# First block of a two-block float32 kernel: nine low weight parts a layer by accumulating transfers, a wider rotation, and the last key scalings ahead of the last rotation

## The chip, the cores and the metric

The kernel runs on one core of one Trainium2 chip. The metric is the device time of one execution in microseconds (us); the time before is the median of three runs.

The core has five engines that run their own instruction lists and wait for one another through semaphores: TensorE (PE, matrix products, with its weight loads as PEld), VectorE (DVE), ScalarE (ACT), GpSimd (POOL) and SyncE (SP, which here only issues transfers). Data comes from the chip's memory by 16 DMA engines that all issuing engines share.

## The reference

Two blocks of two layers each, on one sequence of 256 positions with 1024 features, all in float32. The change is in the first block. Its middle part, the mixer, is this (shortened):

```python
def mixer(h, w_in, ...):
    z = h @ w_in + b_in
    q, k, v, glu_in, gates = jnp.split(z, ...)        # 1536, 1536, 1536, 2048, 2048 wide
    q = apply_rope(rmsnorm(q.reshape(shp), q_norm), cos, sin)   # 24 heads of 64
    k = apply_rope(rmsnorm(k.reshape(shp), k_norm), cos, sin)
    for g, (window, dil) in enumerate(DILATION_GROUPS):
        o, l = dilated_window_attn(q[:, :, g], k[:, :, g], v[:, :, g], dil, window // (2 * dil))
    ...                                               # softmax over the three groups
    y_conv = conv_module(glu_in, conv_w, ...)         # depthwise, 31 taps a channel
    g_attn, g_conv = jnp.split(jax.nn.sigmoid(gates), 2, axis=-1)
    return (g_attn * y_attn + g_conv * y_conv) @ w_out

def first_block(x, ...):
    for l in range(DEPTH):                            # DEPTH = 2
        x = x + 0.5 * swiglu_ffn(rmsnorm(x, ffn1_norm[l]), ...)
        x = x + mixer(rmsnorm(x, mix_norm[l]), ...)
        x = x + 0.5 * swiglu_ffn(rmsnorm(x, ffn2_norm[l]), ...)
        x = rmsnorm(x, final_norm[l])
    return x
```

`apply_rope` takes the halves t1, t2 of each head to t1·cos − t2·sin and t1·sin + t2·cos.

## The kernel before

**Products.** A float32 product is made of three products of rounded parts: every weight w is split into hi (w rounded to the format fp32r) and lo = w − hi, and so is every activation. `mm3` (lines 433 to 435) adds hi·hi, hi·lo and lo·hi in PSUM.

**The weight stream.** The weights come in chunks of 128 partitions by 2048 columns (1 MB), or half of that. Chunk c lies in slot c mod 3 of three tiles: `raw` (as loaded), `hi` and `lo`. For each chunk SP issues the load (`chunk`, line 357) when the low part of chunk c − 3 is made, since that was the last reader of the slot's raw tile. ACT makes hi by a copy (`split`, line 1052) when TensorE has finished chunk c − 3. DVE makes lo by a subtraction (`split`, line 1549). TensorE waits for the count of low parts and uses the chunk. ACT and DVE split two chunks ahead of the one that TensorE is at.

**The stages of a layer's mixer**, by chunk number: 4 chunks of values (VA0), 8 of the gated unit ahead of the convolution (GLU0), 12 of queries and keys (QK0), 2 of values (V0), 8 of gates (GATE0), then projections. A chunk of queries and keys gives a pair of 128-row tiles. In QK step i:

- ACT runs `split` for chunk QK0+i+2 and then `qk_step1(i)`: when TensorE has finished chunk QK0+i it writes the pair, scaled, to `zg` (line 1157) and its squares to `zgsq` (line 1166). At i = 6 and i = 12 it also takes a square root for the norms of six pairs (line 1163).
- SP, once `zg` is there, copies it with the halves of each head exchanged to `zr` (`turn_halves`, line 367, four transfers of 64 KB).
- DVE runs `split` for chunk QK0+i+2, then `rope1(i−2)`: zg·cos (line 1708), zr·sin (line 1709) and their sum into `qk` (line 1711). It then may scale a pair by its norm (`qk_scale`, line 1719), from the norms that TensorE has spread over the partitions (lines 568 and 579). Last come six convolution taps (`some_taps`, line 1746, or 1743 for a channel tile's first tap). The 248 taps of a layer have no fixed place; they are dealt out by constants, 7 for each of six GLU steps, 6 for each QK step, 8 for each V step, 16 for each head step.

**Heads.** When six pairs are scaled, TensorE makes the first score tile (`score_pair`, line 605). Then come eight head steps t. In each TensorE runs `gates_and_values(t)`: gate chunk GATE0+t, in it the values of step t−1 (line 632), and spreads of the late six pairs' norms (`late_spread`, line 590, at k = 4 and k = 7 of the chunk's eight, by the table `late_spread_at`). Then it transposes (line 618) and makes the next scores. DVE adds the mask and takes a minimum (`scaled_min`, line 1725), splits a chunk, inverts the sums (line 1730), scales late pairs and runs taps. ACT runs the exponentials (line 1173), scales them (line 1180), splits a chunk, makes the gate (line 1266) and copies the transposed tiles (line 1185). A late spread of pair c waits until pair c−1 is scaled. At t = 6 TensorE sums the finished convolution for its norm (line 708).

GpSimd has no part in all this. The order on each engine is the order in which the code is written.

## Time and profile before

| | |
|---|---|
| time before, median of 3 runs | 2053.53 us (2047.05 to 2054.88) |
| profiled execution: its time, its span | 2046.14 us, 2044.4 us |
| granted TensorE clock over the span | 0.988 of full |
| PE busy | 1957.5 us (96%) |
| DVE busy | 1534.2 us (75%) |
| ACT busy | 1038.0 us (51%) |
| POOL busy | 0.2 us |
| chain that ended last | PE 70%, DVE 22%, ACT 5%, DMA 2% |

The busy share of PE is modelled: matmuls overlap, so a busy PE may still be short of its peak. The mixer of the first layer runs from about 205 to 520 us of the span, that of the second from about 920 to 1235 us. Both read alike, and the rows below are of the first.

### The profile page before, as it was taken

Reading aid. Unit: us, or ns where it says so; the run is one execution under the profiler, and the core shown is the slowest. Engines: PE = TensorE matmul, PEld = TensorE weight load, DVE = VectorE, ACT = ScalarE, POOL = GpSimd, SP = SyncE. Lnnn points to the kernel's source line nnn. Section 1 sums busy time; section 2 is a strip of 40 time slices with the busy share of each in tenths; the row PEclk is TensorE's granted clock in tenths of the full one; section 3 lists DMA queues with packets and bytes.
Section 4 is the critical chain, followed back from the end, with each engine's and each line's share of the span. In section 5 each row is a group of like instructions: output and inputs, shape, how many; then the busy total and the mean of one; then the engine's idle time right before and its main releaser. Section 6 shows DMA issues by size and latency. Waiting matters only on the chain.

```text
span 2044.4 us, 38994 instructions
## 1 busy us (share of the span) xinstructions
PE 1957.5 (96%) x15906; PEld 1882.4 (92%) x15906; DVE 1534.2 (75%) x2207; ACT 1038.0 (51%) x1322; POOL 0.2 (0%) x4
## 2 busy tenths in 40 slices
PE   7999999799999999999997999999999999999998
PEld 7999998688999999999987889999888999888998
DVE  6556899997765576568999977555787777878776
ACT  5444545365544454444454555444465555565554
POOL 0000000000000000000000000000000000000000
PEclk9999999899999999999998999999999999999999
DMA  6556555224555545555552236555235554334553
GB/s 246 193 185 222 190 189 188 79 76 131 207 205 185 181 142 191 194 207 200 197 181 83 73 126 231 189 185 177 94 124 175 195 185 165 135 124 165 185 185 134
DMA packets 55817, 343.38 MB, mean 168 GB/s; under 512 B 7328, under 2 KB 7584, under 8 KB 18976
## 3 DMA queue, kind: packets, MB, share of 16 engines
q1 hardware_dynamic: 54704, 339.37, 47.6%
q10 hardware_dynamic: 1008, 2.51, 0.3%
q8 instruction: 78, 1.28, 0.2%
q14 instruction: 27, 0.22, 0.0%
HBM read 334.51 MB, written 1.05 MB: 164 GB/s over the span
## 4 chain that ended last, share of the span: by engine, by line
PE 70%; DVE 22%; ACT 5%; DMA 2%; issue 1%; ACTq 0%; DVEq 0%; SPq 0%
PE bank L433 22%; PE bank L435 22%; PE bank L434 22%; DVE lo L1549 7%; DVE cv L1746 6%; ACT hi L1052 2%; DMA raw<-in_w 1%; DVE p_sb L1725 1%; DVE qk L1719 1%; DVE n_lo L1553 1%; DMA x<-in_x 1%; DVE sq L1583 0%; DVE zr L1709 0%; PE bank L821 0%; DVE zg L1708 0%
## 5 line engine op out<-in xcount | busy, mean ns | idle before, releaser
L1549 DVE TENSOR_TENSOR lo<-raw,hi 128x2048 fp32r<-128x2048 f32 (+1 forms) x336 | 715.2, 2129 | 232.8 <-ACT hi L1052 232.2
L433 PE MATMUL bank<-n_hi,hi 128*128 128x256 f32 x2256 | 637.8, 283 | 28.6 <-DVE lo L1773 12.6
L1052 ACT ACTIVATE hi<-raw 128x2048 fp32r<-128x2048 f32 (+1 forms) x336 | 597.4, 1782 | 94.8 <-PE bank L435 81.1
L434 PE MATMUL bank<-n_lo,hi 128*128 128x256 f32 x2256 | 631.7, 280 | 0.0
L435 PE MATMUL bank<-n_hi,lo 128*128 128x256 f32 x2256 | 631.5, 280 | 0.0
L433 PEld LDWEIGHTS bank<-n_hi,hi 128*128 128x128 f32 x2256 | 427.2, 189 | 34.2 <-DVE lo L1773 12.6
L434 PEld LDWEIGHTS bank<-n_lo,hi 128*128 128x128 f32 x2256 | 427.2, 189 | 1.2 <-issue 1.0
L435 PEld LDWEIGHTS bank<-n_hi,lo 128*128 128x128 f32 x2256 | 428.2, 190 | 0.0
L433 PE MATMUL bank<-h_hi,hi 128*128 128x256 f32 x1152 | 337.6, 293 | 7.3 <-DVE h_lo L1553 5.3
L434 PE MATMUL bank<-h_lo,hi 128*128 128x256 f32 x1152 | 328.6, 285 | 0.0
L435 PE MATMUL bank<-h_hi,lo 128*128 128x256 f32 x1152 | 328.3, 285 | 0.0
L433 PE MATMUL bank<-hid_hi,hi 128*128 128x256 f32 x960 | 269.1, 280 | 3.5 <-DVE lo L1549 3.5
L435 PE MATMUL bank<-hid_hi,lo 128*128 128x256 f32 x960 | 268.9, 280 | 0.0
L434 PE MATMUL bank<-hid_lo,hi 128*128 128x256 f32 x960 | 268.8, 280 | 0.0
L433 PEld LDWEIGHTS bank<-h_hi,hi 128*128 128x128 f32 x1152 | 223.4, 194 | 20.6 <-issue 14.4
L434 PEld LDWEIGHTS bank<-h_lo,hi 128*128 128x128 f32 x1152 | 223.9, 194 | 0.5
L435 PEld LDWEIGHTS bank<-h_hi,lo 128*128 128x128 f32 x1152 | 223.6, 194 | 0.0
L1746 DVE SCALAR_TENSOR_TENSOR cv<-upad,prm,cv 128x256 f32<-128x256 f32 x480 | 195.7, 476 | 0.0
L1096 ACT ACTIVATE silu_t<-up_t 128x256 f32<-128x256 f32 x88 | 36.8, 418 | 300.3 <-DVE up_t L1604 300.3
L433 PEld LDWEIGHTS bank<-hid_hi,hi 128*128 128x128 f32 x960 | 181.7, 189 | 3.9 <-DVE lo L1549 3.9
L435 PEld LDWEIGHTS bank<-hid_hi,lo 128*128 128x128 f32 x960 | 182.2, 190 | 0.0
L434 PEld LDWEIGHTS bank<-hid_lo,hi 128*128 128x128 f32 x960 | 181.6, 189 | 0.0
(242 smaller groups left out, 2225.3 us busy)
## 6 DMA issues: line engine op xcount, KB each, us to landing
raw<-in_w SPq DMA_DIRECT2D x286, 1024.0 KB, 4.8
raw<-in_w SPq DMA_DIRECT2D x53, 512.0 KB, 3.9
zr<-zg SPq DMA_DIRECT2D x96, 64.0 KB, 2.9
bv<-in_bv SPq DMA_DIRECT2D x2, 768.0 KB, 6.2
spread<-in_spread SPq DMA_DIRECT2D x2, 768.0 KB, 8.0
x<-in_x ACTq DMA_DIRECT2D x4, 256.0 KB, 10.3
out_x<-sq SPq DMA_DIRECT2D x1, 1024.0 KB, 3.9
const<-in_const ACTq DMA_DIRECT2D x1, 831.5 KB, 14.1
```

Of the source, the lines that this page charges most:

```text
L433: mm(out, w_hi, a_hi, start=start, stop=False, skip_group_check=True)
L434: mm(out, w_hi, a_lo, start=False, stop=False, skip_group_check=True)
L435: return mm(out, w_lo, a_hi, start=False, stop=True, skip_group_check=True)
L1052: fn(hi[:, s, 0:w], raw[:, s, 0:w], ACT.Copy).then_inc(sem["hi"], 1)
L1096: fn(silu_t[:, u, :], gate_of[:, u, 0, :], ACT.Silu).then_inc(sem["silu"], 1)
L1549: v.tensor_tensor(lo[:, s, 0:w], raw[:, s, 0:w], hi[:, s, 0:w].bitcast(F32), ALU.subtract)\
L1553: return v.tensor_tensor(out, full, high.bitcast(F32), ALU.subtract).then_inc(sem[name], 1)
L1719: v.tensor_tensor(t, norm_of, t, ALU.mult).then_inc(sem["qk"], 1)
L1725: v.tensor_tensor_reduce(p_sb[:, e, :], bank[3 + e][:, :], mask_f[:, u % 2, :], -(HD ** -0.5), 3e38, ALU.add, ALU.min, nmx[:, i:i + 1]).th ...
L1746: ins = v.scalar_tensor_tensor(cv[:, t, :], src, w, cv[:, t, :], ALU.mult, ALU.add)
```

## The change

**1. Nine low parts a layer are made without DVE.** For the chunks in `ADDED` (QK0+1, 3, 5, 7, 9, 11 and GATE0, GATE0+2, GATE0+4) ACT writes −hi to the slot's `lo` right after it has written hi. GpSimd then issues a transfer of the same 1 MB chunk out of memory that adds to `lo`, which gives w − hi. TensorE waits for that transfer. SP's next load into the slot waits for ACT's second copy.

**2. The rotation is one product of 1024 columns** for a pair and its turned copy, in one tile `zt` of three buffers, then the sum. The turned copy had two buffers.

**3. Order on DVE.** After a QK step whose split is gone there are 11 taps instead of 6. In the value steps pairs 4 and 5 are scaled ahead of the last rotation. The late norms' reciprocal, the third part of the values and eight taps go behind the first `scaled_min`. The late spreads are dealt out as 1, 2, 2, 1 instead of 2, 2, 1, 1, and the first waits for the values.

```diff
 def late_spread_at(t):
-    return {0: [6, 7], 1: [8, 9], 2: [10], 3: [11]}.get(t, [])
+    return {0: [6], 1: [7, 8], 2: [9, 10], 3: [11]}.get(t, [])
+ADDED = tuple(QK0 + i for i in (1, 3, 5, 7, 9, 11)) + (GATE0, GATE0 + 2, GATE0 + 4)
...
-        def chunk(c, src, half):
-            sp.wait_ge(sem["lo"], cnt.up("lo"))
+        def chunk(c, src, half, after_added=False):
+            if after_added:
+                sp.wait_ge(sem["minus"], cnt.up("minus"))
+            else:
+                sp.wait_ge(sem["lo"], cnt.up("lo"))
...
+        def take_low(c):
+            if c in ADDED:
+                take(f"added{ADDED.index(c) % 2}", 16)
+            else:
+                take("lo")
...
-                if k in (4, 7) and late:
+                if late and (k == 7 or (k == 4 and t)):
+                    if t == 0:
+                        take("v")
                     late_spread(late.pop(0))
...
-        def split(c, half=False):
+        def split(c, half=False, added=False):
...
             fn(hi[:, s, 0:w], raw[:, s, 0:w], ACT.Copy).then_inc(sem["hi"], 1)
+            if added:
+                act.wait_ge(sem["hi"], cnt.at("hi", 1))
+                fn(lo[:, s, 0:w], hi[:, s, 0:w].bitcast(F32), ACT.Copy, scale=-1.0).then_inc(sem["minus"], 1)
...
-            take(f"turn{i % 2}", 64)
-            v.tensor_tensor(zg[:, i % 3, :, :], zg[:, i % 3, :, :], cos, ALU.mult)
-            link(v.tensor_tensor(zr[:, i % 2, :, :], zr[:, i % 2, :, :], sin, ALU.mult))
+            take(f"turn{i % 3}", 64)
+            both = zt[:, i % 3, :, :, :]
+            link(v.tensor_tensor(both, both, turns, ALU.mult))
...
-            for i in range(12):
-                split(QK0 + i + 2)
-                qk_at(i)
-                some_taps(TAPS_QK)
-            for j in range(2):
-                split(V0 + j + 2)
-                qk_at(12 + j)
-                some_taps(TAPS_V)
-            for c in spread_at(13):
-                qk_scale(c)
-            add_values(2, V0 + 1)
+            for i in range(12):
+                split(QK0 + i + 2, added=QK0 + i + 2 in ADDED)
+                if i >= 2:
+                    rope1(i - 2, turns)
+                if i == QK_CHUNKS + 1:
+                    key_rstd(0)
+                for c in spread_at(i - 1):
+                    qk_scale(c)
+                some_taps(TAPS_QK + (5 if QK0 + i + 2 in ADDED else 0))
+            split(V0 + 2, added=V0 + 2 in ADDED)
+            rope1(10, turns)
+            for c in spread_at(11):
+                qk_scale(c)
+            some_taps(TAPS_V)
+            split(V0 + 3, added=V0 + 3 in ADDED)
+            for c in spread_at(12) + spread_at(13):
+                qk_scale(c)
+            rope1(11, turns)
...
             for t in range(8):
                 scaled_min(t)
+                if t == 0:
+                    key_rstd(1)
...
                 inverse_sums(t)
+                if t == 0:
+                    add_values(2, V0 + 1)
+                    some_taps(TAPS_V)
...
+    def pool_program(pool):
+            for n, c in enumerate(ADDED):
+                pool.wait_ge(sem["minus"], cnt.up("minus"))
+                pool.dma_start(lo[:, c % SLOTS, :], d["w1"][l * CHUNKS1 + c], accum_op=ALU.add)\
+                    .then_inc(sem[f"added{n % 2}"], 16)
```

**On DVE, from the second value step to the first minimum of the heads.** Here `lo<-raw,hi` is the split of chunk GATE0+1, `zg`, `zr` and `qk<-zg,zr` the rotation, `qk<-bank,qk` a pair's scaling, `cv` the taps, `rstd` the late norms' reciprocal, `v` the values. Before:

```order
L1549 TENSOR_TENSOR lo<-raw,hi 128x2048
L1708 TENSOR_TENSOR zg<-zg,const 128x512
L1709 TENSOR_TENSOR zr<-zr,const 128x512
L1711 TENSOR_TENSOR qk<-zg,zr 128x512
L1865 RECIPROCAL rstd<-std 128x256
L1719 TENSOR_TENSOR qk<-bank,qk 128x512
L1746 SCALAR_TENSOR_TENSOR cv<-upad,prm,cv 128x256 x2
L1743 TENSOR_SCALAR cv<-upad,prm 128x256 x2
L1746 SCALAR_TENSOR_TENSOR cv<-upad,prm,cv 128x256 x4
L1719 TENSOR_TENSOR qk<-bank,qk 128x512
L1760 TENSOR_TENSOR v<-bank,bv 128x512 x2
L1725 ISA p_sb,small<-bank,mask_f 128x512
```

Now:

```order
L1570 TENSOR_TENSOR lo<-raw,hi 128x2048
L1740 TENSOR_TENSOR qk<-bank,qk 128x512 x2
L1730 TENSOR_TENSOR zt<-zt,const 128x1024
L1732 TENSOR_TENSOR qk<-zt 128x512
L1746 ISA p_sb,small<-bank,mask_f 128x512
```

The reciprocal, eight taps, the values and the last rotation no longer stand ahead of the sixth pair's scaling, for which the first scores wait.

**On DVE, behind that minimum, up to the scaling of the first late pair.** Before:

```order
L1746 SCALAR_TENSOR_TENSOR cv<-upad,prm,cv 128x256 x3
L1730 RECIPROCAL small<-small 128x2
L1746 SCALAR_TENSOR_TENSOR cv<-upad,prm,cv 128x256 x3
L1719 TENSOR_TENSOR qk<-bank,qk 128x512
L1746 SCALAR_TENSOR_TENSOR cv<-upad,prm,cv 128x256 x3
```

Now:

```order
L1882 RECIPROCAL rstd<-std 128x256
L1751 RECIPROCAL small<-small 128x2
L1781 TENSOR_TENSOR v<-bank,bv 128x512 x2
L1767 SCALAR_TENSOR_TENSOR cv<-upad,prm,cv 128x256 x11
L1740 TENSOR_TENSOR qk<-bank,qk 128x512
```

What left the place above stands here, ahead of the late pairs.

**On ACT, two QK steps in a row**, `hi` being the high part and `lo<-hi` the negated copy. Before:

```order
L1052 ACTIVATE hi<-raw 128x2048
L1157 ACTIVATE zg<-bank,qk_bg,prm 128x256 x2
L1166 ACTIVATE zgsq<-bank,prm 128x256 x2
L1052 ACTIVATE hi<-raw 128x2048
L1157 ACTIVATE zg<-bank,qk_bg,prm 128x256 x2
```

Now:

```order
L1066 ACTIVATE hi<-raw 128x2048
L1069 ACTIVATE lo<-hi 128x2048
L1175 ACTIVATE zt<-bank,qk_bg,prm 128x256 x2
L1184 ACTIVATE zgsq<-bank,prm 128x256 x2
L1066 ACTIVATE hi<-raw 128x2048
L1175 ACTIVATE zt<-bank,qk_bg,prm 128x256 x2
```

Every second step has one more copy of 2048 columns, ahead of the pair that TensorE has yet to finish.

## Rows read from the trace of the kernel before

**Rows 1.** Waits of the whole kernel: total us, times, longest.

```profile
PE bank L605 <- DVE qk L1719: 20.8, 2, 10.4
```

**Rows 2.** Windows: length, busy PE, PEld, DVE, ACT, POOL, clock, DMA share, GB/s.

```profile
364.00:372.00 8.00, 3.37 (x17) 2.23 (x15) 7.96 (x15) 0.00 (x0) 0.00 (x0) 0.89 0.38 133
372.00:380.00 8.00, 2.21 (x13) 1.82 (x14) 6.93 (x13) 0.00 (x0) 0.00 (x0) 0.50 0.27 114
```

**Rows 3.** Chain that ended last, ahead of the first scores: start, duration, what.

```profile
364.61 3.17 DVE cv L1746 x8
...
377.13 0.61 DVE qk L1719
377.79 2.08 PE bank L605 x12
```

**Rows 4.** DVE in order of time, QK step 7: start, duration, instruction.

```profile
323.88 2.29 DVE L1549 TENSOR_TENSOR lo<-raw,hi 128x2048 fp32r<-128x2048 f32 x1 [1.72 <-ACT hi L1052]
326.09 0.68 DVE L1708 TENSOR_TENSOR zg<-zg,const 128x512 f32<-128x512 f32 x1
...
328.03 1.74 DVE L1865 RECIPROCAL rstd<-std 128x256 f32<-128x256 f32 x1
```

**Rows 5.** ACT in order of time: splits, and starts of a pair (TensorE just done).

```profile
268.98 1.90 ACT L1052 ACTIVATE hi<-raw 128x2048 fp32r<-128x2048 f32 x1
280.12 1.02 ACT L1157 ACTIVATE zg<-bank,qk_bg,prm 128x256 f32<-128x256 f32 x2 [2.82 <-PE bank L435]
281.75 1.93 ACT L1052 ACTIVATE hi<-raw 128x2048 fp32r<-128x2048 f32 x1
292.41 1.02 ACT L1157 ACTIVATE zg<-bank,qk_bg,prm 128x256 f32<-128x256 f32 x2 [2.98 <-PE bank L435]
294.03 1.92 ACT L1052 ACTIVATE hi<-raw 128x2048 fp32r<-128x2048 f32 x1
305.46 1.02 ACT L1157 ACTIVATE zg<-bank,qk_bg,prm 128x256 f32<-128x256 f32 x2 [2.97 <-PE bank L435]
321.93 1.92 ACT L1052 ACTIVATE hi<-raw 128x2048 fp32r<-128x2048 f32 x1
331.55 1.02 ACT L1157 ACTIVATE zg<-bank,qk_bg,prm 128x256 f32<-128x256 f32 x2 [2.98 <-PE bank L435]
```

**Rows 6.** The page's DMA issues: count, KB each, median us to landing.

```profile
raw<-in_w SPq DMA_DIRECT2D x286, 1024.0 KB, 4.8
zr<-zg SPq DMA_DIRECT2D x96, 64.0 KB, 2.9
```

**Rows 7.** Windows of 1 us behind one load's issue (columns as rows 2).

```profile
299.78:300.78 1.00, 1.00 (x11) 1.00 (x10) 1.00 (x3) 1.00 (x4) 0.00 (x0) 1.00 0.93 344
300.78:301.78 1.00, 1.00 (x10) 1.00 (x9) 1.00 (x4) 1.00 (x1) 0.00 (x0) 1.00 0.99 393
301.78:302.78 1.00, 1.00 (x11) 1.00 (x10) 0.93 (x3) 0.71 (x1) 0.00 (x0) 1.00 0.86 334
302.78:303.78 1.00, 1.00 (x11) 1.00 (x10) 1.00 (x1) 0.00 (x0) 0.00 (x0) 1.00 0.64 191
```

**Rows 8.** Chain again, in the head steps: start, duration, what.

```profile
397.97 0.61 DVE qk L1719
398.62 1.15 PE bank L590 x4
...
463.64 0.84 ACT gate L1266 x2
```

**Rows 9.** DVE in order of time behind the first scores (gap in brackets).

```profile
383.66 0.17 DVE L1730 RECIPROCAL small<-small 128x2 f32<-128x2 f32 x1 [1.15 <-ACT p_sb L1173]
...
385.63 0.69 DVE L1719 TENSOR_TENSOR qk<-bank,qk 128x512 f32<-128x512 f32 x1 [0.63 <-PE bank L590]
...
388.65 0.69 DVE L1719 TENSOR_TENSOR qk<-bank,qk 128x512 f32<-128x512 f32 x1 [1.14 <-PE bank L590]
```

**Rows 10.** A window within the head steps (columns as rows 2).

```profile
412.00:420.00 8.00, 8.00 (x75) 7.47 (x72) 8.00 (x18) 4.21 (x10) 0.00 (x0) 1.00 0.09 15
```

More of the change, by code:

```diff
@@ L402, in sp_program @@
             for c in range(VA0, FFN2_0):
-                chunk(c, d["w1"][l * CHUNKS1 + c], half_chunk_1(c))
+                chunk(c, d["w1"][l * CHUNKS1 + c], half_chunk_1(c), c - SLOTS in ADDED)
                 i = c - QK0 - 5
@@ L407, in sp_program @@
             ffn_stream(l, d["w1"], FFN2_0, CHUNKS1)
-            cnt.end(layer, dict(lo=CHUNKS1, zg=2 * QK_CHUNKS, rope=2 * QK_CHUNKS))
+            cnt.end(layer, dict(lo=CHUNKS1 - len(ADDED), minus=len(ADDED), zg=2 * QK_CHUNKS, rope=2 * QK_CHUNKS))
         for l in range(L):
@@ L445, in gates_and_values @@
             c, out = GATE0 + t, bank[GATE_BANKS[t % 2]]
-            take("lo")
+            take_low(c)
             late = late_spread_at(t)
@@ L456, in gates_and_values, with pairs @@
             last.then_inc(sem["pe"], 1)
-        def pairs(c, out, k0, nk, a_hi, a_lo, start, ready=None, stat_after=None, by_halves=False):
+        def pairs(c, out, k0, nk, a_hi, a_lo, start, ready=None, stat_after=None, by_halves=False, added=False):
             if by_halves:
                 pe.wait_ge(sem["lo0a"], 1)
+            elif added:
+                take_low(c)
             else:
@@ L681, in layer1 @@
                     pe.wait_ge(sem["u"], cnt.at("u", 6 + i))
-                pairs(c, bank[c % 3], 0, KT, h_hi, h_lo, True)
+                pairs(c, bank[c % 3], 0, KT, h_hi, h_lo, True, added=True)
                 qk_tail1(i)
@@ L691, in layer1 @@
             for t in range(8):
-                if t == 0:
-                    take("v")
                 if t >= 2:
@@ L1156, in qk_step1 @@
                     t = qk_tile(i) + j
-                    last = fn(zg[:, i % 3, j, :], src[:, j * S:(j + 1) * S], ACT.Identity, scale=col(P1, "qk_g", qk_gain(i)),
+                    last = fn(zt[:, i % 3, 0, j, :], src[:, j * S:(j + 1) * S], ACT.Identity, scale=col(P1, "qk_g", qk_gain(i)),
                               bias=qk_bg[:, t:t + 1])
@@ L1240, in layer1 @@
                 c = GLU0 + t
-                split(c + 2)
+                split(c + 2, added=c + 2 in ADDED)
                 take("pe")
@@ L1258, in layer1 @@
                 normed_pair(t)
-                split(GATE0 + t + 2, half_chunk_1(GATE0 + t + 2))
+                split(GATE0 + t + 2, half_chunk_1(GATE0 + t + 2), GATE0 + t + 2 in ADDED)
                 if t:
@@ L1542, in link, with split @@
             v.wait_ge(sem["link"], cnt.up("link"))
-        def split(c, half=False):
+        def split(c, half=False, added=False):
             s = c % SLOTS
             w = CW // 2 if half else CW
+            if added:
+                cnt.up("hi")
+                return
             take("hi")
@@ L1841, in layer1 @@
                 c = GLU0 + t
-                split(c + 2)
+                split(c + 2, added=c + 2 in ADDED)
                 take("sig")
@@ L1854, in layer1, with key_rstd @@
                     some_taps(TAPS_GLU)
[L1856 to L1865 removed]
+            turns = const[:, C["cos1"]:C["cos1"] + 2 * S].rearrange("p (h s) -> p h s", h=2)
+            turns = turns.unsqueeze(2).broadcast_to([P, 2, 2, S])
+            def key_rstd(batch):
+                take("qstd")
+                v.reciprocal(rstd[:, batch, :], std[:, 0, :]).then_inc(sem["qrstd"], 1)
+            for i in range(12):
+                split(QK0 + i + 2, added=QK0 + i + 2 in ADDED)
+                if i >= 2:
+                    rope1(i - 2, turns)
+                if i == QK_CHUNKS + 1:
+                    key_rstd(0)
                 for c in spread_at(i - 1):
                     qk_scale(c)
[L1869 to L1879 removed]
+                some_taps(TAPS_QK + (5 if QK0 + i + 2 in ADDED else 0))
+            split(V0 + 2, added=V0 + 2 in ADDED)
+            rope1(10, turns)
+            for c in spread_at(11):
+                qk_scale(c)
+            some_taps(TAPS_V)
[3 more added lines that the diff above has]
+            rope1(11, turns)
             v.wait_ge(sem["mask1"], 16)
@@ L1882, in layer1 @@
                 scaled_min(t)
+                if t == 0:
+                    key_rstd(1)
                 if t:
-                    split(GATE0 + t + 1, half_chunk_1(GATE0 + t + 1))
-                else:
-                    some_taps(3)
+                    split(GATE0 + t + 1, half_chunk_1(GATE0 + t + 1), GATE0 + t + 1 in ADDED)
                 inverse_sums(t)
+                if t == 0:
+                    add_values(2, V0 + 1)
+                    some_taps(TAPS_V)
                 for c in late_spread_at(t):
@@ L2206, in dve_program @@
             cnt.end(before, PER_LAYER2)
+    def pool_program(pool):
+        cnt = Count({})
+        for l in range(L):
+            layer = cnt.begin()
+            for n, c in enumerate(ADDED):
+                pool.wait_ge(sem["minus"], cnt.up("minus"))
+                pool.dma_start(lo[:, c % SLOTS, :], d["w1"][l * CHUNKS1 + c], accum_op=ALU.add)\
+                    .then_inc(sem[f"added{n % 2}"], 16)
+            cnt.end(layer, dict(minus=len(ADDED)))
     with nc.Block() as block:
@@ L2226, in _ @@
             dve_program(v)
+        @block.gpsimd
+        def _(pool):
+            pool_program(pool)
 def _tiles(w, rows, cols):
```

38 lines of the change are left out of this document (15 added, 23 removed).

## The prediction

> **What bounds the kernel now.** The page gives TensorE as busy for 96% of the span and as 70% of the chain, so DVE work that is saved helps only where TensorE waits for it. I read next who waited for whom. One entry stands out: the first scores of each layer wait 10.4 us, twice, for a pair's scaling on DVE [rows 1]. The windows there show what it costs besides: PE is busy 3.4 and 2.2 of 8 us, and the granted clock falls to 0.50, the lower of its two levels (1.2 GHz), after the engine stood idle [rows 2]. The chain shows what holds the scaling back: a DVE that runs without a gap, with taps, a split, a rotation, a reciprocal and eight more taps ahead of it; then come scores that take 2.08 us at the low clock [rows 3]. TensorE was there at 377.79 − 10.4 = 367.4 us, so that is when the scores could start at best. Elsewhere in the queries and keys TensorE sets the pace: the pairs finish 6.5 us apart (292.41 to 305.46 is two steps) and ACT, which follows, waits 2.97 us in each step for TensorE [rows 5].
>
> **The stall.** What leaves DVE ahead of the sixth scaling, counted back from 377.1 us, with a split at 326.09 − 323.88 = 2.2 and a tap at 3.17/8 = 0.40 [rows 3, 4]:
> - QK step 7 no longer waits for ACT's high part: 1.7.
> - Steps 7, 9 and 11 lose a split (2.2) and gain five taps (2.0): 0.2 each, 0.6 in all. So nearly all the split time freed there goes into taps that are taken from the heads.
> - A rotation takes 328.03 − 326.09 = 1.94. One product of 1024 columns isn't in the trace. A third of a rotation, 512 columns, is 0.65, the split's 2048 are 2.2; 1024 columns on that line are 1.2, against 1.3 for the two products replaced. So 0.1 a rotation, six times 0.6; if it saves nothing, the 2 us to spare below cover it.
> - In the value steps: the split of GATE0 2.2, the last rotation 1.9, the reciprocal 1.7, eight taps 3.2.
>
> Together 11.9, so DVE would be there at 365.2, ahead of TensorE's 367.4, with 2 us to spare. Then TensorE's spread for the sixth pair ends last; after it come one scaling (0.6) and the scores, from 368.1 to about 369.2, as the clock has no reason to fall (1.0 to 1.1 instead of 2.08). Before, the scores ended at 379.9. **Gain 10.7 us a layer up to there.**
>
> **The heads.** What left that place stands now behind the first minimum, and I don't expect the heads to get shorter. Before, the second spread of step 1 started 398.62 − 379.87 = 18.75 us behind the first scores' end [rows 8]. Now it waits for late pair 7 and DVE has this more or less to do until then: five more taps 2.0, a reciprocal 1.7, the values 1.3 (two of 512 columns), the rest of the last rotation 0.4; less a split 2.2 and a scaling 0.6. Its gaps there were 1.15 + 0.63 + 1.14 [rows 9]; the new work fills them, but behind the second minimum nothing stands between it and the exponentials, which I put at the same 1.15, with 0.5 for the first: 1.3 less. Together 1.3 later. Behind that DVE's relief (25 taps done early, two splits gone) buys little, for TensorE itself has no gap in these steps: 8.00 of 8 us, like DVE [rows 10]. The two are level there, and taking work from one leaves the other. The last gate stood 463.64 − 379.87 = 83.8 us behind the first scores [rows 8]; I take 0.5 more, as the later steps give back part of the 1.3. **Net 10.2 us a layer, 20.4 in all, if the accumulating transfers cost nothing.** ACT's extra copies (1.9 each) fit into its 2.97 us waits in the queries and keys; in head steps 0 and 2 they delay the transposed tiles' copies by up to 1.3 us, in step 0 beside the wait just counted.
>
> **The accumulating transfers.** This is the term that decides, and no row shows such a transfer. First what it is allowed. For an added chunk ACT needs from the start of the high part 2 × 1.9 = 3.8 us; the transfer then has until TensorE wants the chunk, which is when it finished the one before. From the pairs' starts [rows 5]: QK0+1: 280.12 − 268.98 − 3.8 = 7.3; QK0+3: 292.41 − 281.75 − 3.8 = 6.9; QK0+5, and likewise QK0+7: 305.46 − 294.03 − 3.8 = 7.6; QK0+9: 331.55 − 321.93 − 3.8 = 5.8, since ACT's table load makes its split late; QK0+11: 7.6 or more. A wait ahead of one added chunk lengthens what the next is allowed by as much. The chunks of the heads have more, since a head step is longer; I put 10 on them.
>
> Now what it takes. A 1 MB load lands 4.8 us after its issue [rows 6]. In the windows behind such a load the 16 engines are busy 0.93 + 0.99 + 0.86 + 0.64 = 3.4 us for 1.26 MB (load and turned copies) [rows 7]: 2.8 us for a megabyte, and 2.0 us fixed. The transfer isn't alone: SP's next load waits for the same semaphore as GpSimd, so the two start together and share the engines. If adding costs the engines what a copy does, both land after 2.0 + 2 × 2.8 = 7.6 us. If it costs them twice, 2.0 + 3 × 2.8 = 10.4. Below, the floor is a lone copy's 4.8. GpSimd's making of the transfer has no row either; SP's issue is short, and I put 0.6 on it. I take **8.2 us**, the copy's price in company plus the issue, because the load is the nearest row: same bytes, same partitions.
>
> With 8.2 the waits are 0.9, 0.4, 0.2, 0.4, 2.0 and 0: 3.9 us a layer, all on TensorE's path, since TensorE sets the pace there. With 7.6: 2.5. With 10.4: 10.5. With 12: 15.3. The clock is not at stake in waits this short.
>
> On that price the Trainium skill has a rule that speaks against the change: the page "Collectives: The Full Stack", section "The bandwidth ceiling: the fold count and why AG ≠ RS ≠ AR", says that a reducing transfer runs at half the rate of a copying one because it reads two sources. No row here can show it. By it the landing would be about 11 us, the waits about 12 us a layer, and the change would lose some 4 us in all; the second rival works that case out from rows.
>
> **The sum.** 2 × (10.2 − 3.9) = 12.6 us. Against the profiled execution's 2046.1 that gives 2033.5. That execution is 7.4 us below the median of the runs shown (2053.5); the comparison is of medians, so I predict 2053.5 − 12.6, rounded to **2041 us**.
>
> **Rivals.**
> - *The transfers are hidden.* The two share less than I think, or land in 6 us: waits 0.2 a layer, gain 20: 2033 by the median, 2026 by the profiled execution. For it: the engines are busy 3.4 us of a 6.5 us step [rows 5, 7], and the loads have steps of slack while only the sum is urgent. Against: both start on one semaphore.
> - *Reading twice costs twice.* Landing 9.5 to 11.9 us: waits 7.8 to 15, so between 5 us gained and 10 lost: 2049 to 2063, around 2054. For it: the engines are busy 0.99 at 393 GB/s [rows 7], so a copy already fills them, and the sum has to read SBUF too. Then the stall is gone and small waits have taken its place.
> - *The adding is slow, or GpSimd is* (the other side). It decides from a landing of 12 us: 2 × (15.3 − 10.2) = 10 us slower, 2064. At 16 us the waits are 8.7, 0.4, 8.0, 0.4 and 9.8, and GATE0 adds some 5: 32 a layer, 44 us slower in all, 2097. The place is the start of the odd QK chunks, the price all on TensorE, and DVE's relief worth nothing. For it: nothing in the trace; against it: nothing either.
> - *It doesn't do what it says.* DVE still ends last at the sixth scaling, because turned copies land late beside the new traffic: at most a few us, within the bound.
>
> **How the numbers follow.** About 0.5%, or 10 us, is what a measurement of this kernel can tell from no change. Forecast, landing 7.3 to 9.4 us: 0.42, of it two thirds over 10 us gained (0.28) and 0.14 within. Transfers hidden: 0.19, faster. Twice the cost: 0.17, within. Slow: 0.18, slower, with 0.01 more from the last rival, whose other 0.03 are within. That makes faster 0.47, same 0.34, slower 0.19. The range goes from 2028, between what the hidden case gives by the two bases, to 2062, the far end of the double price; it leaves out most of the slow case.
>
> **What would show it.** Right: no wait of 10 us ahead of the first scores, clock at full there, scores at about 1.1 us, PE waits at the odd QK chunks of 0 to 2 us, first scores to last gate about 84 us. The landing time of GpSimd's transfers is the first number to read: under 7.6 the hidden case, over 10.2 no gain, over 12 a loss. Wrong in another way: if DVE still ends last at the first scores, my count of what stood ahead of them is off; if the heads got shorter, TensorE wasn't as near to its own pace as I read it; if ACT had become late, the pairs would start later than TensorE's ends.

## The result: 0.9% slower, and the profile after

The changed kernel takes **2068.6 us** (median of 4 runs, 2063.0 to 2071.3), the kernel before beside it 2050.3 us (median of 4, 2045.9 to 2054.9). The ratio is **1.0087**, 95% interval 1.0061 to 1.0114. I had forecast 2041 us with a range of 2028 to 2062: the sign was wrong, and the time lies 6.6 us above the range. The profiled execution took 2063.0 us with a span of 2061.2 us; that of before took 2046.1 us and 2044.4 us.

The page after has the number to read first, the landing of GpSimd's transfers, beside the plain loads' (count, KB each, median us from issue to landing; [rows 6] has those of before):

```profile
raw<-in_w SPq DMA_DIRECT2D x286, 1024.0 KB, 4.9
lo<-in_w POOLq DMA_DIRECT2D x18, 1024.0 KB, 11.3
```

The waits of TensorE over the whole kernel (total us, times, longest) stand against [rows 1]; the last row is of layer 1, at the first scores:

```profile
PE bank L439 <- DMA lo<-in_w: 27.7, 9, 5.0
PE bank L607 <- DVE qk L1740: 5.8, 2, 2.9
...
PE bank L622 <- DVE qk L1740: 0.8, 1, 0.8
```

The 10.4 us wait ahead of the first scores is gone, 0.8 us is left. In its place stand 27.7 us of waiting for the sums, and 2.9 us a layer at the late spread of head step 1. DVE is busy for 1494.1 us instead of 1534.2 us, and nothing of that shows in the time.

Where it is lost is told by three marks in layer 1: ACT's copies of the twelve pairs, DVE's minima and ACT's gates. The last two numbers ahead of the semicolon are the first and the last start. First before, then after:

```profile
L1157 ACT ACTIVATE zg<-bank,qk_bg,prm x24: 554/561/566, 280.1 to 353.5; 128x256 f32<-128x256 f32 x24
L1725 DVE CUSTOM_DVE_ANT_0 p_sb<-bank,mask_f x16: 674/680/690, 380.0 to 456.3; 128x512 f32<-128x512 f32 x16
L1266 ACT ACTIVATE gate<-bank,gate_hb x16: 453/466/475, 389.4 to 464.0; 128x256 f32<-128x256 f32 x16
```

```profile
L1175 ACT ACTIVATE zt<-bank,qk_bg,prm x24: 550/557/563, 280.0 to 371.9; 128x256 f32<-128x256 f32 x24
L1746 DVE CUSTOM_DVE_ANT_0 p_sb<-bank,mask_f x16: 682/692/706, 388.3 to 461.8; 128x512 f32<-128x512 f32 x16
L1283 ACT ACTIVATE gate<-bank,gate_hb x16: 454/466/476, 397.1 to 472.2; 128x256 f32<-128x256 f32 x16
```

Both start the pairs at 280. The queries and keys then take 91.9 us instead of 73.4: **18.5 us lost**. From the last pair to the first minimum it is 16.4 us instead of 26.5: **10.1 us gained**. From there to the last gate it is 83.9 against 84.0. The sum is 8.3 us lost in this layer (192.2 us against 183.9 from the first pair to the last gate); layer 2 gives 8.3 too (192.1 against 183.8), together 16.6 us. The spans differ by 16.8, but that they agree so well is partly chance: between the two stretches the changed kernel is 5.8 us slower and behind the second 5.5 us faster. The change touches neither place; the two traces differ there in TensorE's pace (last section).

Windows of 1 us in the middle of the first sum, and behind it (columns as rows 2):

```profile
278.00:279.00 1.00, 1.00 (x11) 1.00 (x10) 1.00 (x2) 0.00 (x0) 0.00 (x0) 1.00 0.96 197
280.00:281.00 1.00, 0.00 (x0) 0.00 (x0) 1.00 (x4) 0.99 (x3) 0.00 (x0) 1.00 0.96 205
...
285.00:286.00 1.00, 1.00 (x8) 1.00 (x8) 1.00 (x3) 0.50 (x1) 0.19 (x1) 0.62 1.10 334
286.00:287.00 1.00, 1.00 (x6) 1.00 (x6) 0.94 (x3) 0.00 (x0) 0.68 (x1) 0.50 0.49 127
287.00:288.00 1.00, 1.00 (x7) 1.00 (x6) 0.00 (x0) 0.00 (x0) 0.00 (x0) 0.50 0.95 313
288.00:289.00 1.00, 1.00 (x8) 1.00 (x7) 0.00 (x0) 0.00 (x0) 0.00 (x0) 0.67 1.06 381
289.00:290.00 1.00, 1.00 (x10) 1.00 (x10) 0.00 (x0) 0.00 (x0) 0.00 (x0) 1.00 1.03 328
```

Two things are to be seen. While the sum alone is under way, the 16 engines are full (0.96) at 197 to 205 GB/s; a plain load filled them (0.99) at 393 GB/s [rows 7]. The Trainium skill, "Collectives: The Full Stack", section "The bandwidth ceiling: the fold count and why AG ≠ RS ≠ AR", has a reducing transfer at half the rate of a copying one, for the steps of a collective between ranks, and gives the two source reads as the reason. The rate in this trace agrees, and the landing of about 11 us was nearer than mine; that the second read is the reason is something that no run here can separate. And TensorE, which stood idle from 280.0 on, gets going at 284.4 at full clock, but from about 285.3 to 288.6 the granted clock is at the lower of its two levels (1.2 GHz), and 6 to 8 products start in a microsecond instead of 10.

So my theory after the result was: a sum costs the engines twice a copy and lands after 11.3 us; the waits are 13.3 us a layer, and the clock that falls behind them costs 18.5 − 13.3 = 5.2 us more. The rest of the change does what I forecast. The rivals: GpSimd's queue is slow, not the adding; the load in company is the main part; the clock's fall costs nothing that the waits don't; the reordering is a loss of its own.

### The profile page after: what moved, and what is told of

It is laid out like the page before. It is cut to its first block, busy times and chain, and to the rows that moved or that the text cites. A ratio compares the mean times of both kernels' runs of the same rounds, so it can differ in the third digit from the quotient of the medians.

```text
span 2061.2 us, 38984 instructions
## 1 busy us (share of the span) xinstructions
PE 1961.8 (95%) x15906; PEld 1888.6 (92%) x15906; DVE 1494.1 (72%) x2165; ACT 1072.5 (52%) x1340; POOL 15.9 (1%) x22
## 4 chain that ended last, share of the span: by engine, by line
PE 74%; DVE 11%; ACT 6%; DMA 6%; issue 2%; ACTq 0%; DVEq 0%; POOL 0%; SPq 0%; POOLq 0%
PE bank L439 24%; PE bank L440 23%; PE bank L441 23%; DVE lo L1570 4%; DMA lo<-in_w 4%; ACT hi L1066 3%; DMA raw<-in_w 1%; ACT lo L1069 1%; DVE n_lo L1574 1%; DMA x<-in_x 1%; PE bank L649 0%; DVE cv L1767 0%; PE bank L622 0%; DVE sq L1604 0%; PE bank L835 0%
## 5 line engine op out<-in xcount | busy, mean ns | idle before, releaser
L1570 DVE TENSOR_TENSOR lo<-raw,hi 128x2048 fp32r<-128x2048 f32 (+1 forms) x318 | 674.4, 2122 | 265.3 <-ACT hi L1066 264.8
L439 PE MATMUL bank<-h_hi,hi 128*128 128x256 f32 x1152 | 341.0, 296 | 34.8 <-DMA lo<-in_w 27.7
## 6 DMA issues: line engine op xcount, KB each, us to landing
lo<-in_w POOLq DMA_DIRECT2D x18, 1024.0 KB, 11.3
x<-in_x ACTq DMA_DIRECT2D x4, 256.0 KB, 10.2
```

The source lines that it names most:

```text
L439: mm(out, w_hi, a_hi, start=start, stop=False, skip_group_check=True)
L1570: v.tensor_tensor(lo[:, s, 0:w], raw[:, s, 0:w], hi[:, s, 0:w].bitcast(F32), ALU.subtract)\
```

## The experiments

All stages are read by the same three marks. Times are us; "pairs" is from the first to the last pair's copy, "stall" from there to the first minimum, "heads" from there to the last gate, all in layer 1. "Layer 2" is the whole stretch from the first pair to the last gate there. The ratio is to the kernel before on the same chip, with its interval. The diffs are against the changed kernel where nothing else is said. "Copy, no sum" leaves out the adding and "half sums" the second half of each sum; both are for timing alone. One thing goes with `ADDED` and isn't visible in the short diffs: the five extra taps of a QK step are dealt only where that step's split is gone. The kernels without sums in the queries and keys therefore leave 25 more taps a layer to the heads than the changed kernel, "one pair, three gates" 20.

| kernel | pairs | stall | heads | sum | layer 2 | landing of a sum | ratio |
|---|---|---|---|---|---|---|---|
| before | 73.4 | 26.5 | 84.0 | 183.9 | 183.8 | | 1 |
| changed | 91.9 | 16.4 | 83.9 | 192.2 | 192.1 | 11.3 | 1.0087 (1.0061 to 1.0114) |
| order only | 73.3 | 19.6 | 88.8 | 181.7 | 181.3 | | 0.9982 (0.9967 to 0.9996) |
| three gate sums | 73.3 | 16.9 | 86.4 | 176.6 | 176.7 | 11.1 | 0.9915 (0.9889 to 0.9941) |
| copy, no sum | 78.3 | 16.4 | 83.8 | 178.5 | 180.8 | 7.9 | 0.9946 (0.9929 to 0.9962) |
| load held | 85.8 | 16.7 | 82.5 | 185.0 | 187.5 | 10.0 | 1.0040 (1.0026 to 1.0054) |
| half sums | 80.3 | 16.4 | 82.6 | 179.3 | 180.0 | 8.3 | 0.9971 (0.9954 to 0.9989) |
| kept warm, 14/13/16 | 92.0 | 16.4 | 85.2 | 193.6 | 192.9 | 11.3 | 1.0081 (1.0054 to 1.0109) |
| kept warm, 9/8/10 | 86.8 | 16.5 | 84.4 | 187.7 | 188.7 | 11.4 | 1.0033 (1.0023 to 1.0044) |
| one pair, three gates | 78.7 | 16.7 | 84.7 | 180.1 | 181.3 | 11.0 | 0.9972 (0.9958 to 0.9986) |
| nine sums, old order | 92.5 | 21.8 | 82.1 | 196.4 | 197.4 | 11.4 | 1.0142 (1.0102 to 1.0181) |
| three gate sums, old order | 73.4 | 23.8 | 82.2 | 179.4 | 179.5 | 11.1 | 0.9975 (0.9959 to 0.9992) |
| six gate sums | 73.4 | 16.4 | 85.4 | 175.2 | 173.6 | 11.2 | 0.9923 (0.9893 to 0.9953) |
| six, taps moved | 73.3 | 16.4 | 87.1 | 176.8 | 176.3 | 11.2 | 0.9941 (0.9924 to 0.9958) |

**What a sum costs: copying instead.**

```diff
-pool.dma_start(lo[:, c % SLOTS, :], d["w1"][l * CHUNKS1 + c], accum_op=ALU.add)
+pool.dma_start(lo[:, c % SLOTS, :], d["w1"][l * CHUNKS1 + c])
```

> The changed kernel with one difference: GpSimd's transfer copies the chunk from HBM on to the low part without adding. Left out: the sum with the negated high part, so the low parts of the nine chunks are wrong; bytes, queue, waits and order are the same. Theory 1 (adding costs the DMA engines twice, since they read SBUF as well): landing falls from 11.3 to 7.5 to 8.2 us, PE's waits for it from 13.8 to 3 to 4 us a layer, no fall of the clock at the odd chunks, and the whole is 26 to 32 us faster than the changed kernel, near 2020 to 2026 by a profile or 0.987 to 0.990 of before. Theory 2 (GpSimd's queue or its making of the transfer is what is slow): landing 10.5 us or more, time as the changed kernel's, 1.006 to 1.011 of before.

The landing and the waits of layer 1:

```profile
lo<-in_w POOLq DMA_DIRECT2D x18, 1024.0 KB, 7.9
...
PE bank L439 <- DMA lo<-in_w: 3.1, 4, 1.8
```

Same queue, same bytes from HBM, same company: 7.9 us. GpSimd's own issue takes 0.5 us instead of 0.9, so 0.3 of the 3.4 us between the two landings are in issuing; the rest is the transfer. So it is the adding, not GpSimd's queue, that makes 11.3 of it. The queue's line on the page (packets, MB, share of the 16 engines' span) says so directly, the changed kernel first, then the copying one:

```profile
q0 software_dynamic: 2592, 18.88, 4.6%
```

```profile
q0 software_dynamic: 2592, 18.88, 2.4%
```

The packets and bytes are the same, and they hold the engines twice as long: 0.046 × 2061.2 / 18 = 5.3 us a megabyte for a sum, 0.024 × 2039.8 / 18 = 2.7 for a copy. In its windows the engines are full at 418 to 451 GB/s, twice what the sum reaches; two of them:

```profile
275.00:276.00 1.00, 1.00 (x11) 1.00 (x10) 1.00 (x4) 0.94 (x1) 0.00 (x0) 1.00 0.99 418
277.00:278.00 1.00, 1.00 (x10) 1.00 (x10) 1.00 (x3) 0.00 (x0) 0.00 (x0) 1.00 1.04 418
```

This is also the kernel that my forecast described: landing 8.2, waits 3.9 a layer, 12.6 us gained. It measures 7.9 plus the issue's delay, 3.1 and 5.2 us of waits in the two layers, and 8.4 us gained by the stages, 11 by the ratio. One thing of theory 1 failed: the clock did fall once, behind the longest wait of layer 1 (0.79 in 332 to 340 us). By the ratios it is 29 us faster than the changed kernel, within the 26 to 32 expected, by the stages 25; the ratio to before that I had put beside them, 0.987 to 0.990, was worked out wrongly (1.0087 less 1.4% is 0.995).

**Bytes: half a sum.**

```diff
-pool.dma_start(lo[:, c % SLOTS, :], d["w1"][l * CHUNKS1 + c], accum_op=ALU.add)
+pool.dma_start(lo[:, c % SLOTS, 0:CW // 2], d["w1"][l * CHUNKS1 + c][:, 0:CW // 2], accum_op=ALU.add)
```

> The changed kernel with GpSimd adding only the first half of each chunk, 512 KB. Left out: the sum in the second half, so the low parts there are wrong. It tells the fixed part of the landing from the part by bytes. Theory (3.2 us fixed with GpSimd's issue, 5.6 us a megabyte for a sum, 2.8 for the load beside it): landing 8.2 to 8.8 us, PE's waits for it 5 to 7 us a layer. Rival (most of the 11.3 us is fixed): landing 10 us or more.

```profile
lo<-in_w POOLq DMA_DIRECT2D x18, 512.0 KB, 8.3
```

Half a megabyte less takes 11.3 − 8.3 = 3.0 us off: 6.0 us a megabyte for a sum. The copy says the same from the other side: 11.3 − 7.9 = 3.4 more than the 2.8 of a plain megabyte is 6.2. Both are read from landings and lie somewhat above the 5.3 of the queue's line. That leaves 5.2 us for what is fixed and for the load beside it. Waits were 5.1 us in layer 1, as expected (4.4 in layer 2).

**The company: the load held back.**

```diff
 if after_added:
-    sp.wait_ge(sem["minus"], cnt.up("minus"))
+    n = ADDED.index(c - SLOTS) % 2
+    sp.wait_ge(sem[f"added{n}"], cnt.up(f"added{n}", 16))
+    cnt.up("minus")
```

> The changed kernel with one difference: SP's load into the slot that an accumulating transfer reads from is held until that transfer has landed, not only until the negated high part is there. So the sum has the 16 engines to itself. Theory 1 (each engine pays twice for a sum, and shares with the load): landing 2.0 + 2 x 2.8 + 0.3 = 7.9 to 8.6 us, still about 200 GB/s at a full share of the engines; PE's waits for it fall to 4 us a layer or less, the whole 20 to 28 us faster than the changed kernel if the held loads still land in time. Theory 2 (the company of the load doesn't matter): landing 10.5 us or more. A third outcome: landing short, but the loads, 8 us later, make ACT's high parts late, and the gain is lost there.

The third outcome, in part. The first rows are of layer 1 alone, 262 to 460 us (issues, then TensorE's waits); the last is the page's, for the whole kernel:

```profile
lo<-in_w POOLq DMA_DIRECT2D x9, 1024.0 KB, 8.8
PE bank L441 <- DMA lo<-in_w: 9.2, 5, 2.9
...
lo<-in_w POOLq DMA_DIRECT2D x18, 1024.0 KB, 10.0
```

With the load held a sum lands after 8.8 us in this stretch, so the load beside it makes some 2.5 of the 11.3 us, and at most 8.8 − 6.1 = 2.7 are fixed. In layer 2 the median is 10.1 us, with waits of 8.7 us there. For the held load only moves: it meets the next sum. The windows show the two loads behind the first sum, at 418 and 434 GB/s, still running as GpSimd issues the second (POOL busy at 286):

```profile
285.00:286.00 1.00, 1.00 (x11) 1.00 (x10) 1.00 (x4) 1.00 (x1) 0.00 (x0) 1.00 0.99 418
286.00:287.00 1.00, 1.00 (x10) 1.00 (x10) 1.00 (x3) 0.45 (x1) 0.25 (x1) 1.00 1.04 434
```

The waits fell from 13.8 to 9.2 us, not to 4. The kernel is 7.2 and 4.6 us a layer better than the changed one and still slower than before.

**The clock: spare products ahead of the waits.**

```diff
+WARM = {1: 14, 5: 13, 9: 16}
...
 elif added:
+    if c in (QK0 + 1, QK0 + 5, QK0 + 9):
+        spare_products(WARM[c - QK0])
     take_low(c)
```

> The changed kernel with 14, 13 and 16 spare products on an unused bank ahead of TensorE's three long waits in the queries and keys (chunks QK0+1, +5, +9), so that the engine isn't idle while the sum lands. Theory (of the 18.5 us a layer that the queries and keys grew by, 13.3 is waiting and 5.1 the low clock after it): the granted clock stays at 1.00 in the windows behind the three waits, the stretch from the first to the twelfth pair falls from 91.4 to 86 to 87 us, and the whole is 8 to 11 us faster than the changed kernel: ratio to before 1.003 to 1.005. Rival (the waits alone make the loss; the clock's fall is hidden behind something else): clock at 1.00, but the stretch stays within 1 us of 91.4 and the ratio at 1.008 or more.

By the numbers the rival was met: clock at 1.00, pairs 92.0 us, ratio 1.0081. But its reason, that the low clock costs nothing, doesn't follow, for this kernel has a fault of its own. The first spare products, in order of time:

```profile
279.94 6.21 PE L507 MATMUL bank<-const 128*128 128x256 f32 x28
```

Fourteen calls are 28 instructions and last 6.2 us, where the wait was 4.4. The spare products had become the wait. So I made them shorter: 9, 8 and 10.

> As the kernel with spare products, but with 9, 8 and 10 of them in place of 14, 13 and 16. In the earlier one 14 took 6.2 us, 0.44 each, against a wait of 4.4 us: the spare products themselves ended 1.8, 1.8 and 2.2 us after the sums, 5.8 us a layer, about what the clock gave back. Now they take 4.0, 3.5 and 4.4 us and end ahead of the sums. Theory (the low clock costs 5 us a layer): no fall of the clock, pairs one to twelve 86 to 87.5 us apart (91.4 in the changed kernel), 8 to 10 us faster than it in all, ratio to before 1.003 to 1.005. Rival (the clock's fall costs nothing that shows): 91 us and ratio 1.008 again.

Windows of 8 us behind the first and the third long wait, the changed kernel first, then this one:

```profile
284.00:292.00 8.00, 7.62 (x50) 7.49 (x52) 2.94 (x8) 1.61 (x2) 0.87 (x1) 0.79 0.95 285
348.00:356.00 8.00, 6.79 (x41) 6.79 (x42) 6.41 (x14) 0.61 (x1) 0.86 (x1) 0.66 1.05 327
```

```profile
284.00:292.00 8.00, 7.47 (x61) 6.95 (x61) 3.09 (x8) 3.08 (x5) 0.87 (x1) 1.00 0.95 283
348.00:356.00 8.00, 8.00 (x66) 7.15 (x65) 5.56 (x14) 3.55 (x5) 0.00 (x0) 1.00 1.06 283
```

The landing is unchanged (11.4), the clock is full, and the pairs take 86.8 us instead of 91.9: **5.1 us were the clock's in layer 1**. In layer 2 the same products give back 3.6 us (87.7 instead of 91.3), there too at 1.00 in every window. The ratio falls from 1.0087 to 1.0033. Spare products kept the clock up in both kernels, but they paid only where they ended ahead of what TensorE waited for.

**The order alone.**

```diff
-ADDED = tuple(QK0 + i for i in (1, 3, 5, 7, 9, 11)) + (GATE0, GATE0 + 2, GATE0 + 4)
+ADDED = ()
```

> Parts 2 and 3 of the change alone: 1024-wide rotation, last scalings first, the new tables of taps and late spreads; no chunk's low part is made by a transfer, DVE splits all of them. My theory (the whole loss of the changed kernel is the waits for accumulating transfers and the clock that falls in them): no PE wait for a DMA at the odd chunks of the queries and keys, the pairs start 6.5 us apart again, clock at full there; DVE has three splits more ahead of the sixth scaling than the changed kernel, so the first scores start near 370 to 372 us of the trace (before 377.79), and the whole is 8 to 16 us faster than before: ratio 0.992 to 0.996. Rival (the reordering itself costs something in the heads that the accumulated waits hid): first scores as early, but first scores to last gate clearly above 84 us, and a ratio of 0.997 or more.

The theory was right up to the first scores: there is no wait for a sum in the queries and keys, the scores start at 370.8, and the first minimum comes at 373.0, 7.0 us earlier than before. For the whole the rival was right: the heads take 88.8 us, 4.8 longer than before, and the ratio of 0.9982 lies beyond its 0.997. TensorE's waits there, 262 to 475 us:

```profile
PE bank L622 <- DVE qk L1740: 3.4, 1, 3.4
PE bank L607 <- DVE qk L1740: 2.5, 1, 2.5
PE bank L722 <- DVE cv L1767: 2.4, 1, 2.4
```

Work that is only moved behind the first scores comes back in the heads, where DVE is full [rows 10]. What pays for it in the changed kernel are two things of like size. The next kernel shows the first: with the sums for the gate chunks the heads go from 88.8 to 86.4. The step from there to 83.9 comes with the sums in the queries and keys, and I put it down to the 25 taps that DVE does early there: the wait of 2.4 us for the convolution (`cv`) is gone with them, and with only 5 of them ("one pair, three gates") it is down to 0.4 and the heads to 84.7. No run moves the taps alone.

**Sums where there is time for them.**

```diff
+ADDED = (GATE0, GATE0 + 2, GATE0 + 4)
```

> As the changed kernel, but only the three low parts of the gate chunks are made by accumulating transfers; those of the queries and keys are split on DVE. My theory: a transfer lands 11.3 us after its issue here too, and the gate chunks allow 10 us or more, so that TensorE waits under 1 us for it; the first scores start some 2 us earlier than with all splits on DVE, near 368 to 370 us of the trace; 14 to 20 us faster than before in all: ratio 0.990 to 0.993. Rival (accumulating transfers hurt wherever they stand, by what they take from the loads): PE waits of some us for loads or turned copies near the gate chunks, ratio no better than without any such transfer.

All as in the theory. The landing is as long as ever, and TensorE hardly notices; layer 1 again (in layer 2 two waits of 1.7 us together):

```profile
lo<-in_w POOLq DMA_DIRECT2D x3, 1024.0 KB, 10.9
...
PE bank L439 <- DMA lo<-in_w: 0.9, 2, 0.7
```

**This version beats both kernels: 2033.0 us, ratio 0.9915.** The first minimum comes at 370.3, 2.7 us earlier than with the order alone, and the heads are 2.4 shorter.

One chunk of the queries and keys added to it shows that the allowance is what decides:

```diff
+ADDED = (QK0 + 5, GATE0, GATE0 + 2, GATE0 + 4)
```

> Three gate chunks and one chunk of the queries and keys, QK0+5, by accumulating transfer. The allowance of the prediction's rule is 7.6 us, the landing with its issue 11.6: one wait of 4.0 us a layer. If the low clock comes behind a single wait of this size too, it costs 1 to 2 us more: pairs up to the twelfth 5 to 6 us later than with gate chunks only, 10 to 12 us in all, ratio to before 0.996 to 0.998. Rivals: landing is shorter here since no other sum is about, wait under 2 us; or a wait of 4 us alone leaves the clock as it is, 8 us in all, ratio 0.9955.

```profile
PE bank L439 <- DMA lo<-in_w: 3.8, 1, 3.8
```

The rule gave 4.0 and the trace has 3.8; the pairs take 5.4 us more. The other 1.6 I put down to the clock, which reads 0.79 in the window behind this one wait (308 to 316 us). In layer 2 the wait is 4.4 and the pairs take 6.6 more. The ratio is 0.9972, as expected.

Six gate chunks, one behind the other (a third semaphore orders them):

```diff
+ADDED = tuple(GATE0 + i for i in range(6))
```

> As with three gate chunks only, but all of the first six gate chunks, GATE0 to GATE0+5, get their low part by an accumulating transfer (a third semaphore orders them). A head step is some 10.6 us long, the engines need 5.6 us for a sum and 2.8 for a load: 8.4 us, so it fits by my theory, with waits of 0 to 1 us a chunk. DVE loses three more splits, 6.6 us a layer, and TensorE's waits for DVE in the heads (2.7 + 2.4 + 1.2) go: 4 to 8 us faster in all than with three, ratio to before 0.987 to 0.990. Rival (sums one behind the other collide with each other and with the loads): waits of 2 us or more for transfers in each head step, slower than with three gate chunks.

By the stages it is 1.4 and 3.1 us a layer better than with three, 4.5 in all, at the low end of what was expected; by the ratio, 0.9923 against 0.9915, the two can't be told apart, and the expected 0.987 to 0.990 was missed. In layer 1 a wait of 2.4 us at L607 stayed (0.8 in layer 2), and 2.5 us of waits for sums came in each layer. I tried to take the former away:

```diff
 if t == 0:
     add_values(2, V0 + 1)
-    some_taps(TAPS_V)
-for c in late_spread_at(t):
-    some_taps(3)
+for n, c in enumerate(late_spread_at(t)):
+    if t != 1 or n:
+        some_taps(3)
     qk_scale(c, True)
-some_taps(TAPS_HEAD - 3 * len(late_spread_at(t)) if t < 6 else 8 * TAPS)
+more = 3 if t == 1 else 2 if t >= 2 else 0
+some_taps(TAPS_HEAD + more - 3 * len(late_spread_at(t)) if t < 6 else 8 * TAPS)
```

> Six gate chunks by accumulating transfer, and taps moved: the eight taps of head step 0 go two each into steps 2 to 5, and the scaling of late pair 7 stands ahead of its three taps. TensorE's wait of 2.4 us a layer at the late spread of step 1 is for that scaling (it ended at 388.9 us of the trace), and DVE has slack in the later steps since three splits are gone. Theory: that wait goes, 2 to 5 us less in all than with six gate chunks alone, ratio to before 0.988 to 0.991. Rival (DVE's taps are late at the end of the heads instead): a wait of TensorE for the convolution's sum of 1 us or more a layer, ratio unchanged at 0.992.

The rival held. The wait at L607 went, but waits for sums grew and the one for the convolution came back; by the stages the kernel is 1.6 and 2.7 us a layer slower than with six gate chunks alone:

```profile
PE bank L439 <- DMA lo<-in_w: 4.0, 4, 2.0
PE bank L722 <- DVE cv L1767: 2.4, 1, 2.4
```

**What the moves are worth.** The old order from the value steps on, with nine sums and with three:

```diff
-    return {0: [6], 1: [7, 8], 2: [9, 10], 3: [11]}.get(t, [])
+    return {0: [6, 7], 1: [8, 9], 2: [10], 3: [11]}.get(t, [])
...
+if t == 0:
+    take("v")
...
-if late and (k == 7 or (k == 4 and t)):
-    if t == 0:
-        take("v")
+if late and k in (4, 7):
...
-for c in spread_at(12) + spread_at(13):
-    qk_scale(c)
 rope1(11, turns)
+key_rstd(1)
+for c in spread_at(12):
+    qk_scale(c)
+some_taps(TAPS_V)
+for c in spread_at(13):
+    qk_scale(c)
+add_values(2, V0 + 1)
...
 if t == 0:
-    key_rstd(1)
+    some_taps(3)
...
-if t == 0:
-    add_values(2, V0 + 1)
-    some_taps(TAPS_V)
```

> The changed kernel with all nine sums and the wide rotation, but in the order of before from the value steps on: last rotation and reciprocal ahead of the last scalings, eight taps and the values ahead of the first minimum, late spreads dealt 2, 2, 1, 1. By my count DVE had 10.4 us too much ahead of the first scores, of which rotation, reciprocal and taps make 6.8, and three splits that are gone, less five taps each, little; but TensorE now comes 17 us later. So DVE is there in time for most of it: first scores 0 to 4 us later than in the changed kernel, heads 2 to 4 us shorter, the whole within 4 us of the changed kernel, ratio 1.006 to 1.011. Rival (the moves were worth their 7 us here too): first scores 6 us or more later, ratio 1.012 or more.

> Accumulating transfers for GATE0, GATE0+2 and GATE0+4 only, wide rotation, but the order of before from the value steps on. Beside the kernel with the same three sums in the new order it tells what the moves are worth where no sum holds TensorE back. Theory (the moved rotation, reciprocal and taps are 6.8 us of DVE ahead of the first scores, and DVE ends last there): first minimum 5 to 7 us later than 370.3 of the trace, heads 2 to 4 us shorter than 86.4, so 4 to 8 us slower in all than with the new order, ratio to before 0.994 to 0.996. Rival (without the sums in the queries and keys the order no longer matters): ratio 0.991 to 0.992.

With nine sums the first minimum comes 5.8 us later, and TensorE waits 5.7 us ahead of the first scores; the heads give 1.8 back. So the moves are worth 4.2 us in layer 1 in the changed kernel too (5.3 in layer 2), and the ratio of 1.0142 is the rival's. I had expected them to be worth nearly nothing there, since TensorE came so much later; but DVE can't use that time: it waits for ACT's high parts then (18.5 us in 262 to 385 us of the changed kernel, against 3.8 before). That its last steps ahead of the scores also hang on the last pairs, like TensorE's, I read from the order of the code. With three sums the first minimum comes 6.7 us later, the heads give 4.2 back, and the kernel is slower by 2.8 us a layer, 5.6 in all, within the 4 to 8 expected. The ratio is 0.9975 instead of 0.9915, above the 0.994 to 0.996 that was expected; its interval, 0.9959 to 0.9992, just touches that range.

## Why the prediction was wrong, point by point

- **The stall.** Forecast: 10.7 us gained up to the first scores. Measured, behind the last pair: 10.1. The sign of what comes last was right too: 0.8 us of the 10.4 is left. For the count of what left DVE the changed kernel is a weak test, since its last pair comes 18.4 us later. The kernel with three gate sums, where TensorE comes as before, is a better one. There the count, less the wait in step 7 and the 0.6 of the splits, has the last scaling start at 377.1 − 9.6 = 367.5 us; it starts at 367.8, and the scores at 368.6 take 1.15 us. So the count held, though it has a slip of 0.2 us: step 11 splits the second chunk of values, which is not in `ADDED`, so only steps 7 and 9 lose a split. The product of 1024 columns takes 1.22 us where I had 1.2.
- **The heads.** Forecast: 0.5 longer. Measured: 83.9 against 84.0 in layer 1, 84.4 against 83.9 in layer 2. The wait at the late spread of step 1 is 2.9 us where I had 1.3, and what the heads gave back behind it was more too. So the number was right by terms that cancelled: with the order alone the heads are 4.8 us longer, and the relief that I said "buys little" gave back 4.9 in layer 1, 2.4 by the gate sums and 2.5 most likely by the 25 taps done early.
- **The allowances.** With 11.3 us and 0.3 from ACT's end to the issue, 11.6, the rule gives waits of 4.3, 0.4, 3.6, 0.4, 5.4 and 0, together 14.1. The trace has 4.4, 0, 4.0, 0, 4.9 and 0, together 13.3, and 0.4 at GATE0. The rule was right to within a microsecond; it was fed the wrong landing.
- **The landing: the step that failed.** "I take **8.2 us**, the copy's price in company plus the issue, because the load is the nearest row". It was 11.6. The load was the nearest row in bytes and partitions, not in what the engines do: by the landings a sum takes them some 6.1 us a megabyte, a copy 2.8 (by the queue's line 5.3 and 2.7). The row that spoke to this stood in my own rival: the engines were full at 393 GB/s [rows 7], so whatever else they had to do for a sum was likely to take time of its own. I gave that case 0.17, and the copy's price more than twice that. In waits it is 13.3 us a layer instead of 3.9.
- **The clock: the second step.** "The clock is not at stake in waits this short." It is, and it was another 5.1 us in layer 1 and some 4 in layer 2 (3.6 came back there with spare products). With the price of the second rival this took the result out of its 2049 to 2063: by my own working waits of 13.3 lose 2 × (13.3 − 10.2) = 6.2 us; with all that the pairs grew by, waits and clock, it is 18.5 + 17.9 − 20.4 = 16.0, against the measured 16.6 of the two stretches. I had the very pattern in front of me, 0.50 behind the wait that was to go [rows 2], and used it for the gain but not for the loss.
- **The base.** I subtracted from 2053.5, the median of three runs. Over all runs of before in these comparisons medians were 2044.9 to 2050.3, so the kernel before stands nearer to its profiled 2046.1. This doesn't bear on the sign.

What stays open: when exactly the clock falls. It fell behind each wait of 3.8 us or more that I looked at, where the load was held behind one of 2.9 (0.79 in the windows 308 to 324), with half sums behind one of 2.3 (0.50 in 341 to 342), in the copying kernel even behind one of 1.8 (0.79 in 332 to 340). It did not fall behind one of 2.0 where the load was held (1.00 in 276 to 292) nor behind one of 2.1 with half sums (1.00 in 284 to 292). So the length of the wait alone doesn't decide it.

## What to carry to other kernels

An accumulating transfer is priced by how long it holds the DMA engines, here twice as long as a copy of the same bytes: 11.3 us for a megabyte in company of a load, so it belongs only where the consumer is that far away, with whatever it replaces counted as nothing if the engine relieved isn't the bound. Before a split, a copy or a sum is moved to a transfer, work out for each consumer the time from the last input to its use; those below the landing become waits. And a wait of some 4 us on TensorE is to be booked with 1 to 2 us for the clock behind it: three of them cost 5.1 and 3.6 us in the two layers here.

## What the runs showed of the hardware that I had not expected

**TensorE's pace at full clock is one of two.** In the long loops of the feed-forward parts the products start at one of two rates, with the granted clock at 1.00 and no waits, and they keep it for a whole stretch of some 160 us. The same loop of layer 1, first in the kernel before, then with three gate sums (the number in brackets behind PE's busy time counts the products in 20 us):

```profile
760.00:780.00 20.00, 20.00 (x179) 20.00 (x178) 13.79 (x14) 8.22 (x10) 0.00 (x0) 1.00 0.63 234
```

```profile
760.00:780.00 20.00, 20.00 (x172) 20.00 (x171) 12.68 (x11) 7.75 (x9) 0.00 (x0) 1.00 0.50 177
```

179 against 172 is 4%, or 6 us a stretch. The stretch between layer 1's last gate and layer 2's first pair takes 990.4 − 464.0 = 526.4 us in the kernel before and 1004.4 − 472.2 = 532.2 in the changed one, and each kernel has two fast stretches among the six of the feed-forward parts, not the same two. It would account for much of the scatter of the runs, though I have no trace of two runs of one kernel to show it. For the change it says: compare stretches, not spans, when it is a matter of a few microseconds. What chooses the pace is open.

**GpSimd's issue.** For a sum it is 0.86 to 1.01 us long (0.87 in the mean of the 18), for a plain copy 0.54 in the mean, and it starts 0.3 us after ACT's copy has ended. With it, a sum has at most 2.7 us fixed (8.8 − 6.1), a plain load from SP 2.0 by the prediction's working from [rows 6, 7].
